# A mixture-of-experts encoder step on one Trainium2 core: row spreading in one pass, banks emptied into a row buffer, a shorter router

## The chip, the cores and the metric

One NeuronCore of a Trainium2 chip (trn2) runs the whole program. The metric is the device time in microseconds, as the median of several executions. PE is TensorE, ACT ScalarE, DVE VectorE, POOL GpSimd and SP the engine whose queue issues most DMAs.

## What is computed

The kernel is one step of a streaming encoder for 256 prompt rows and 32 sample rows (288 in all), width 2048, float32. What matters here is the end of the layer:

```python
x = x + mixed @ w_o                                   # "W_O"
h = rmsnorm(x, norm2_g)
g_idx = argmax(h @ wg + bg)                           # 1 of 4 groups per row
e_val, e_idx = top_k(sub[g_idx], 2)                   # 2 of its 4 experts
combine = one_hot(e_id) * softmax(e_val) * p_g
for e in range(16):                                   # ff = 512
    gate, up = split(h @ wu[e], 2)                    # wu[e]: 2048 x 1024
    out = out + combine[:, e:e+1] * ((silu(gate) * up) @ wd[e])   # wd[e]: 512 x 2048
y = rmsnorm(x + out, final_norm_g)
```

## The kernel before

Five engines run programs of their own, in order, and meet at semaphores only. The dense stages come first: input projections, recurrence, attention, the two gated products (`gated` and `gates`, last of all for `w_pa`), then W_O. The 16 experts follow.

**Precision.** A product keeps float32 accuracy by splitting an operand: ACT writes the rounded high part (`hi`, L893), DVE the remainder (`lo`, L1766 and L1769), and PE runs float32r matmuls over the parts. In the expert stage a 1 MB *piece* of weights is loaded to one of 5 `raw` slots and split in two *halves*; four `sH`/`sL` buffers hold split halves. There are 8 up pieces (U) and 4 down pieces per expert. An up half is 4 matmuls (`up_half`), a split down half (D) 6 (`three`). `NATIVE = [(2, 3)]` names the down pieces that aren't split: for these (N) PE multiplies the raw weights in float32 (`whole`, L1330), and ACT and DVE have nothing to do.

**Order.** `STREAM` is the list of the 192 pieces, made from `PLANS`: string `PLANS[e]` interleaves the U of expert e+1 with the D and N of e; "-" puts in the down pieces of e-1 that are still open. `NTH[t]` counts the split halves ahead of half t. Every engine walks this same list, and other work is tied to places in it (`GL_AT`, `SILU_AT`, `AT_AT`, `ROUND_AT`, `META_AT`, `ROWS_AT`, `DONE_AT`). An engine that waits at one place holds up all that is behind it.

**Groups.** The experts are done in 4 groups of 4. For a group, four *gather* rounds bring its at most 96 rows into `xsH`/`xsL`, and eight *spread* rounds put them transposed into `hgs`, 64 slots per expert: here four rounds for experts 0 and 1, four for 2 and 3, each of 8 matmuls with 128 columns. ACT drains both banks of a round (`drain`). For group g+1 four gathers run while expert 1 of group g has its downs, four spreads at expert 2 and four at expert 3. Group 0 has its four gathers, `meta_turn`, four spreads and `row_turn` ahead of the stream, and four spreads in it.

**An expert's turn.** After its last up half ACT and DVE make the gate and the product (`gl`, `silu`, `actHL`), PE moves them to row order (`remap`, L1412), and ACT and DVE copy them out as `atH`, `atL` (split) and `atF` (for N).

**The end of a group.** The output of a group lies in four PSUM banks `out4`. ACT squares them (`finish`, L960), DVE adds, ACT takes the root (`finish_root`, L965), DVE scales all four banks (`finish_rows`, L1914) and frees them with `yo_ready`; POOL writes the rows with two indirect DMAs. PE waits for `yo_ready` before the next group's first down piece (`residual`, L1405).

**The router.** DVE works on a [96, 3, 20] tile of logits in a chain of small dependent instructions: `first_max` on the group logits, selection of the group's four, `first_max` twice on these. PE then ranks the picks with float32 matmuls (L1305, L1308).

Of the kernel before, what the change touches and what calls it, by code (L numbers as in the profile page):

```python
# [22 lines left out]
P = 128  # L23
D = 2048
KT = D // P
# [60 lines left out]
CUT = [e for e in range(NE) if len(NATIVE[e]) < FM]  # L86
NCUT = [sum(1 for x in CUT if x < e) for e in range(NE + 1)]

# [72 lines left out]
def build(nc, x_prompt, x_sample, cache_k, cache_v, state_conv, state_lru, norm1_g, w_in, conv_w,  # L161
# [19 lines left out]
    ones = sb("ones", [P, P])  # L181
    before = sb("before", [P, P])
# [6 lines left out]
    eps_t = sb("eps_t", [TB, 1])  # L189
    prm = sb("prm", [P, P])  # L190
# [99 lines left out]
    lgT = sb("lgT", [40, T])  # L290
    end2 = here[0]
# [28 lines left out]
    r4 = sb("r4", [TB, 8, FT, 4])  # L320
    r1 = sb("r1", [TB, 6, FT, 1])
    psel = sb("psel", [TB, FT, 4, 4])
    picks = sb("picks", [TB, FT, 20])
# [15 lines left out]
    atH = sb("atH", [P, 2, CAP], F32R)  # L339
    atL = sb("atL", [P, 2, CAP], F32R)  # L340
    atF = sb("atF", [P, FM, CAP])
    end3 = here[0]
    assert max(end1, end2, end3) <= nc.sbuf_usable_end, (end1, end2, end3, nc.sbuf_usable_end)
# [21 lines left out]
    with ExitStack() as ctx:  # L365
        def sem(name):
# [55 lines left out]
                                                    sem("routed"))  # L422
        G_ready, meta_ps, R_ready, idx_ready = sem("G_ready"), sem("meta_ps"), sem("R_ready"), sem("idx_ready")
# [7 lines left out]
        atH_ready, atL_ready = sem("atH_ready"), sem("atL_ready")  # L431
        sqy_ready, ssqy_ready, rmsy_ready, yo_ready = (sem("sqy_ready"), sem("ssqy_ready"), sem("rmsy_ready"),
# [5 lines left out]
        def round_banks(q):  # L438

            if q < 8:  # L440
                return trio[q % 3]
            return pair[0] if q % ROUNDS // 4 == 1 else pair[1]
# [241 lines left out]
        def _(a):  # L684
# [93 lines left out]
            def gates(base, m0):  # L778
                def body(i):
                    for b in range(2):  # L780
# [6 lines left out]
                        a.sem_inc(acc_used[0], 1)  # L787
                        ahead(base, 4, i, 2 * b + 1)
                peeled(a, KT // 2, body)

            gates(T_PB, 0)
# [72 lines left out]
            gates(T_PA, KT)  # L864


            for q in range(4):
                a.wait_ge(mix_ready, KT + 4 * (q + 1))
                a.activation(hH[:, 4 * q:4 * q + 4, :], mixed[:, 4 * q:4 * q + 4, :], ACT.Copy)\
                 .then_inc(mixsplit_s, 1)  # L870
# [37 lines left out]

            a.wait_ge(xr_in, 48)
# [16 lines left out]
            a.wait_ge(logit_ps, KT)  # L926
            a.activation(lgT[:, :], bank[4][0:40, 0:T], ACT.Copy).then_inc(lgT_ready, 1)
            a.wait_ge(ssq_ready, FT + 1)
            a.activation(rms[:, :], ssq[:, :], ACT.Sqrt, bias=eps_t[:, :], scale=1.0 / D).then_inc(rms_ready, 1)
            x1_hi(KT - 1, tail)  # L930

            a.wait_ge(top_ready, 1)
            a.activation(r4[:, 1, :, :], r4[:, 0, :, :], ACT.Exp).then_inc(ge_ready, 1)
            a.wait_ge(dd_ready, 1)
            a.activation(r1[:, 1, :, :], r1[:, 0, :, :], ACT.Exp).then_inc(ed_ready, 1)


            def drain(q, c):

                n, r = q // ROUNDS, q % ROUNDS  # L940
                a.wait_ge((turnA_ps, turnB_ps)[c], q + 1)
                src = round_banks(q)[c]
                if r < 4:
                    a.activation((xsH, xsL)[c][:, 512 * r:512 * (r + 1)], src[0:CAP, :], ACT.Copy)\
                     .then_inc((outA, outB)[c], 1)
                else:
                    k, e = 4 * (r % 4) + 2 * c, 2 * (r // 4 - 1)
                    a.activation(hgs[:, k:k + 2, e:e + 2, :, :].rearrange("p k e h s -> p k (e h s)"),
                                 src[:, :].rearrange("p (k c) -> p k c", k=2), ACT.Copy)\
                     .then_inc((outA, outB)[c], 1)  # L950
# [17 lines left out]
            for q in range(8):  # L968
# [3 lines left out]
            rows(0, bank[6])  # L972
            for i in range(HALVES, NSPLIT):
                for e in range(NE):
# [16 lines left out]
                    if i == AT_AT[e]:  # L991
# [4 lines left out]
                        if e in CUT:  # L996
                            a.activation(atH[:, :, :], src[:, 0:2, :], ACT.Copy).then_inc(atH_ready, 1)
                        m0 = NATIVE[e][0]
                        a.activation(atF[:, m0:, :], src[:, m0:, :], ACT.Copy).then_inc(atF_ready, 1)
                for q, t in enumerate(ROUND_AT):  # L1000
                    if t is not None and i == NTH[t] + 4:
                        drain(q, 0)
                        drain(q, 1)
                for g in range(NG - 1):
                    if i == NTH[ROWS_AT[g]] + 5:
                        rows(g + 1, pair[0][1])
                    if i == NTH[DONE_AT[EPG * g + EPG - 1]] + 3:
                        need(a, y_out, 32 * g)
                        a.wait_ge(eh_done, DONE_AT[EPG * g + EPG - 1])
                        finish(g, g)  # L1010
                    if i == NTH[DONE_AT[EPG * g + EPG - 1]] + 6:
                        finish_root(g, g)
                expert_split(i)
            a.wait_ge(y_out, 32 * (NG - 1))
            a.wait_ge(eh_done, HALF_N)
            finish(NG - 1, NG - 1)
            finish_root(NG - 1, NG - 1)

            a.wait_ge(routed, 1)
            n = a.value_load(cnt_i[0:1, 0:1], min_val=0, max_val=T + ES)  # L1020
            with a.If(n > CAP):
                def again(v, first, width):

                    with a.Fori(0, NG) as g:
# [4 lines left out]
                        with a.Fori(0, width) as w:  # L1029
# [9 lines left out]
                            with a.Fori(0, EPG) as j:  # L1039
                                x = EPG * it + j  # L1040
                                for s in range(PU + PD):
                                    if s == PU:
# [11 lines left out]
                                        a.activation(atF[:, :, :],  # L1054
# [23 lines left out]
        def _(pe):  # L1078
# [221 lines left out]

            pe.wait_ge(picks_ready, 1)
# [748 lines left out]
```

## Time and profile before

| | |
|---|---|
| Median of 3 runs | 1850.07 us (1849.16 to 1851.13) |
| Profiled execution, its own time | 1847.03 us |
| Its span, first to last instruction | 1845.1 us |
| Mean granted TensorE clock | 0.978 |
| PE / DVE / ACT busy | 93% / 61% / 56% |
| Expert stream, first up matmul to last down matmul | 1260.85 to about 1830.4 us |

The span is what the views of the trace show; about 2 us lie outside it. The stream is 31% of the span and has other limits than the stages ahead of it, so it is read by itself.

### The profile page before, as it was taken

The numbers are of one execution on the slowest core, as the hardware profiler recorded it, in microseconds if no ns is written. First come the engines' busy times: TensorE is split into PE (matmuls) and PEld (weight loads), VectorE is DVE, ScalarE is ACT, GpSimd is POOL, SyncE is SP. The second block draws the span as 40 slices with busy tenths as digits, with TensorE's granted clock in tenths as the row PEclk, the third lists the DMA queues.
The fourth block names the chain that finished last, engine by engine and source line by source line (L and its number), as shares of the span: only waits on it lengthen the run. The fifth ranks groups of instructions, "written<-read, shape, count | busy, mean of one in ns | idle before, by whom it ended". The sixth has DMA issues, their size and how long they took to land.

```text
span 1845.1 us, 28902 instructions
## 1 busy us (share of the span) xinstructions
PE 1721.5 (93%) x10867; PEld 1505.3 (82%) x10867; DVE 1120.3 (61%) x1410; ACT 1025.3 (56%) x1500; POOL 134.1 (7%) x176
## 2 busy tenths in 40 slices
PE   5999989999999999999999989988998999899896
PEld 5999989999989888988899989976665676566553
DVE  5888874434444444444344455456887887886883
ACT  6666663333344444344333345557788787787873
POOL 2555430000000000000000000000000000000000
PEclk9999999999999999999999999988999999899898
DMA  7555545566554455445755654525899899899993
GB/s 196 146 171 166 147 140 169 151 180 185 165 172 131 130 173 165 124 141 134 191 162 156 182 174 122 193 99 182 336 373 362 327 378 361 325 372 360 345 389 157
DMA packets 418892, 393.55 MB, mean 213 GB/s; under 512 B 19168, under 2 KB 376896, under 8 KB 409664
## 3 DMA queue, kind: packets, MB, share of 16 engines
q1 hardware_dynamic: 407152, 383.04, 62.3%
q10 hardware_dynamic: 10432, 4.79, 1.0%
q0 software_dynamic: 1232, 4.72, 0.9%
q8 instruction: 46, 0.75, 0.2%
q14 instruction: 30, 0.25, 0.0%
HBM read 385.38 MB, written 11.08 MB: 215 GB/s over the span
## 4 chain that ended last, share of the span: by engine, by line
PE 72%; DVE 11%; ACT 8%; issue 6%; DMA 2%; POOL 1%; ACTq 0%; SPq 0%; DVEq 0%; POOLq 0%
PE bank L1114 13%; PE bank L1115 13%; PE bank L1116 13%; PE bank L1330 5%; PE bank L1337 4%; PE bank L1339 4%; DVE sL L1766 4%; ACT sH L893 2%; PE bank L1277 2%; PE bank L1278 2%; PE bank L1279 2%; ACT wH L691 2%; PE bank L1316 1%; PE bank L1319 1%; PE bank L1322 1%
## 5 line engine op out<-in xcount | busy, mean ns | idle before, releaser
L691 ACT ACTIVATE wH<-ring 128x1024 fp32r<-128x1024 f32 x320 | 335.9, 1059 | 539.5 <-PE bank L1116 479.7
L1557 DVE TENSOR_TENSOR wL<-ring,wH 128x1024 fp32r<-128x1024 f32 x320 | 388.0, 1230 | 375.5 <-ACT wH L691 367.5
L1114 PE MATMUL bank<-hH,wH 128*128 128x288 f32 x1792 | 536.7, 300 | 5.8 <-ACTq L753 2.7
L1115 PE MATMUL bank<-hL,wH 128*128 128x288 f32 x1792 | 530.8, 296 | 0.0
L1116 PE MATMUL bank<-hH,wL 128*128 128x288 f32 x1792 | 530.0, 296 | 0.0
L1766 DVE SCALAR_TENSOR_TENSOR sL<-raw,prm,sH 128x1024 fp32r<-128x1024 f32 x256 | 318.3, 1280 | 84.9 <-ACT sH L893 83.6
L1114 PEld LDWEIGHTS bank<-hH,wH 128*128 128x128 f32 x1792 | 339.2, 189 | 13.0 <-issue 7.0
L1115 PEld LDWEIGHTS bank<-hL,wH 128*128 128x128 f32 x1792 | 339.1, 189 | 0.4
L1116 PEld LDWEIGHTS bank<-hH,wL 128*128 128x128 f32 x1792 | 338.8, 189 | 0.0
L893 ACT ACTIVATE sH<-raw,prm 128x1024 fp32r<-128x1024 f32 x256 | 283.2, 1146 | 56.7 <-PE bank L1339 33.9
L1337 PE MATMUL bank<-sH,hgs 128*128 128x512 f32 x512 | 183.8, 441 | 38.0 <-DVE sL L1766 36.4
L1339 PE MATMUL bank<-sL,hgs 128*128 128x512 f32 x512 | 166.5, 407 | 0.0
L1337 PEld LDWEIGHTS bank<-sH,hgs 128*128 128x128 f32 x512 | 91.6, 196 | 89.2 <-DVE sL L1766 63.1
L1114 PE MATMUL bank<-oH,wH 128*128 128x288 f32 x512 | 150.4, 294 | 3.1 <-DVE oL L1654 3.1
L1115 PE MATMUL bank<-oL,wH 128*128 128x288 f32 x512 | 151.2, 295 | 0.0
L1116 PE MATMUL bank<-oH,wL 128*128 128x288 f32 x512 | 151.0, 295 | 0.0
L1339 PEld LDWEIGHTS bank<-sL,hgs 128*128 128x128 f32 x512 | 100.5, 196 | 24.5
L1330 PE MATMUL bank<-raw,atF 128*96 128x512 f32 x256 | 115.3, 592 | 0.0
L1114 PEld LDWEIGHTS bank<-oH,wH 128*128 128x128 f32 x512 | 96.4, 188 | 3.4 <-issue 3.4
L1115 PEld LDWEIGHTS bank<-oL,wH 128*128 128x128 f32 x512 | 96.4, 188 | 0.0
L1116 PEld LDWEIGHTS bank<-oH,wL 128*128 128x128 f32 x512 | 96.3, 188 | 0.0
L1769 DVE TENSOR_TENSOR sL<-raw,sH 128x1024 fp32r<-128x1024 f32 x64 | 77.9, 1224 | 17.5 <-ACT sH L893 16.8
(309 smaller groups left out, 2141.2 us busy)
## 6 DMA issues: line engine op xcount, KB each, us to landing
raw<-in_expert_w_up SPq DMA_DIRECT2D x128, 1024.0 KB, 7.2
ring<-in_w_in SPq DMA_DIRECT2D x112, 1024.0 KB, 6.0
raw<-in_expert_w_down SPq DMA_DIRECT2D x64, 1024.0 KB, 7.0
ring<-in_w_pb SPq DMA_DIRECT2D x16, 1024.0 KB, 8.5
ring<-in_w_pa SPq DMA_DIRECT2D x16, 1024.0 KB, 8.6
ring<-in_w_o SPq DMA_DIRECT2D x16, 1024.0 KB, 5.5
cK<-in_cache_k SPq DMA_DIRECT2D x16, 256.0 KB, 2.9
cV<-in_cache_v SPq DMA_DIRECT2D x16, 256.0 KB, 3.3
```

The source lines that it names most:

```text
L691: a.activation(wH[2 * (slot % 2) + half][:, :, :], ring[slot][:, 8 * half:8 * half + 8, :], ACT.Copy).then_inc(hi_ready, 1)
L893: a.activation(sH[buf][:, :], raw[slot][:, 1024 * half:1024 * (half + 1)], ACT.Copy, scale=scale)\
L1114: pe.matmul(dst, hi, rH[:, k, :], start=(k == 0), stop=False)
L1115: pe.matmul(dst, hi, rL[:, k, :], start=False, stop=False)
L1116: ins = pe.matmul(dst, lo, rH[:, k, :], start=False, stop=(k == KT - 1))
L1277: pe.matmul(dst, hi, hH[:, k, :], start=(k == 0), stop=False, skip_group_check=True)
L1330: ins = pe.matmul(out4[nb][0:CAP, :], atF[:, m, :], raw[slot][:, nb * 512:(nb + 1) * 512], start=False, stop=stop, skip_group_check=True)
L1337: pe.matmul(banks[c][:, :], w, hi[:, c * 512:(c + 1) * 512], start=(k == 0), stop=False)
L1339: ins = pe.matmul(banks[c][:, :], w, lo[:, c * 512:(c + 1) * 512], start=False, stop=(k == KT - 1))
L1557: v.tensor_tensor(lo[:, :, :], ring[slot][:, 8 * half:8 * half + 8, :], hi[:, :, :].bitcast(F32), ALU.subtract).then_inc(lo_ready, 1)
L1766: v.scalar_tensor_tensor(sL[buf][:, :], src, g2[:, 2 * s + half:2 * s + half + 1], sH[buf][:, :].bitcast(F32), ALU.mult, ALU.subtract).the ...
L1769: v.tensor_tensor(sL[buf][:, :], src, sH[buf][:, :].bitcast(F32), ALU.subtract)\
```

## The change

- `gates` and `gated` take the split of `mixed` for W_O into their last iteration: three quarters ahead of the last product's end, the fourth behind it.
- ACT gets four small activations (`warm`) which place the table of the next function (Sqrt, Exp, Silu, Sqrt) earlier. The copy `lgT` goes from ACT to DVE.
- The router's `first_max` runs on the group logits and on all four groups' logits in one [96, 15, 4] tile: 13 dependent steps to `picks`, on 60 elements a row. `picks`, `ones`, `before` become bfloat16; a semaphore `cnt_ps` of its own follows the three count products.
- A spread round has 4 matmuls with 256 columns, for all four experts and two row blocks. Later groups have all eight spreads at expert 2 of the group before, two halves apart. Group 0 has 4 gathers and 3 spreads ahead of the stream, 5 spreads at halves 2 to 10, and `row_turn` at half 12. `meta_turn` goes ahead of the fourth gather. In the stream's first five spreads ACT drains one bank and DVE the other; for later groups ACT drains both.
- At a group's end ACT squares a bank (`square_bank`) and DVE at once multiplies it by the gain into `yo` (`gain_bank`), which frees it (`scaled_ready`). The root's factor is applied to `yo` afterwards, by ACT on one half and DVE on the other. For the last group banks 0 and 1 start when half a piece is still to come.
- The plans change: a group's last down piece now falls into the next plan, and the six U in a row at a group's start become four with an N among them. The last expert has no N.

```diff
-PLANS = ["UUUUDUDUDUU", "UU-UDUUDUUDU", "UU-UDUUDUUDU", "UU-UDUDUDUDUU"] * NG
-PLANS[NE - 2] = "UU-UDUUUDUU"
-NATIVE = [(2, 3)] * NE
+PLANS = ["UU-UUDUDUDUU", "UU-UDUUDUUDU", "UU-UDUUDUUUD", "UU-UDUUDUUDU"] * NG
+PLANS[0], PLANS[NE - 2] = "UUUUDUDUDUU", "UU-UDUUUDUU"
+NATIVE = [(2, 3)] * (NE - 1) + [()]
...
-ROUND_AT = [None] * 8 + [2, 5, 8, 11]
+FIRST_ROWS = 12
+ROUND_AT = [None] * 7 + [2, 4, 6, 8, 10]
 for _g in range(NG - 1):
-    for _j in (1, 2, 3):
-        ROUND_AT += [DOWN_AT[EPG * _g + _j] + 3 * r for r in range(4)]
+    ROUND_AT += [DOWN_AT[EPG * _g + 1] + 3 * r for r in range(4)]
+    ROUND_AT += [DOWN_AT[EPG * _g + 2] + 2 * r for r in range(8)]
...
+                        if last and b == 1:
+                            for q in range(4):
+                                mixed_hi(q)
                         ahead(base, 4, i, 2 * b + 1)
...
+            a.activation(warm[:, 0:1], eps_t[:, :], ACT.Sqrt)
             a.wait_ge(xr_in, 48)
             part(0)
...
+            def square_bank(g, nb):
+                a.activation(yo[:, 512 * nb:512 * (nb + 1)], out4[nb][0:CAP, :], ACT.Square,
+                             accum_out=ssqy[:, g, nb:nb + 1]).then_inc(sqy_ready, 1)
+            def scale_half(g):
+                a.wait_ge(scaled_ready, 4 * (g + 1))
+                a.wait_ge(root_ready, g + 1)
+                a.activation(yo[:, 1024:], yo[:, 1024:], ACT.Copy, scale=rmsy[:, g, 2:3]).then_inc(yo_ready, 2)
...
                     else:
-                        for kk in range(2):
-                            ins = spread(dst[:, 256 * kk:256 * (kk + 1)].rearrange("p (e h s) -> p e h s", e=2, h=2),
-                                         4 * (r % 4) + 2 * c + kk, 2 * (r // 4 - 1), 2)
+                        ins = spread(dst[:, :].rearrange("p (e h s) -> p e h s", e=EPG, h=2),
+                                     2 * (r - 4) + c, 0, EPG)
...
-            for q in range(4):
-                round(q)
-            pe.wait_ge(meta_ready, 1)
-            meta_turn(0, bank[6])
-            for q in range(4, 8):
+            for q in range(7):
+                if q == 3:
+                    pe.wait_ge(meta_ready, 1)
+                    meta_turn(0, bank[6])
                 round(q)
-            pe.wait_ge(R_ready, 1)
-            row_turn(bank[6], ms[:, 0, 4:9])
...
                 if t == UP_AT[e]:
-                    if j == 0:
-                        pe.wait_ge(outA, ROUNDS * g + 8)
-                        pe.wait_ge(outB, ROUNDS * g + 8)
...
+                    if j == 0 and g > 0 or j == 1:
                         pe.wait_ge(outA, ROUNDS * (g + 1))
                         pe.wait_ge(outB, ROUNDS * (g + 1))
...
                     if j == 0:
-                        need(pe, yo_ready, 4 * g)
+                        if g == 0:
+                            pe.wait_ge(es_ready, 1)
+                        need(pe, scaled_ready, 4 * g)
...
+            def gain_bank(g, nb):
+                v.wait_ge(sqy_ready, 4 * g + nb + 1)
+                if nb == 3:
+                    finish(g, g)
+                c = slice(512 * nb, 512 * (nb + 1))
+                v.tensor_tensor(yo[:, c], out4[nb][0:CAP, :], gain[:, c], ALU.mult).then_inc(scaled_ready, 1)
+            def finish_rows(g):
+                v.wait_ge(rmsy_ready, g + 1)
+                v.reciprocal(rmsy[:, g, 2:3], rmsy[:, g, 1:2]).then_inc(root_ready, 1)
+                v.wait_ge(root_ready, g + 1)
+                v.wait_ge(scaled_ready, 4 * g + 2)
+                v.tensor_scalar(yo[:, 0:1024], yo[:, 0:1024], rmsy[:, g, 2:3], None, ALU.mult).then_inc(yo_ready, 2)
```

## Rows read from the trace of the kernel before

**Rows 1.** The page, busy tenths in 40 slices of 46 us.
```profile
DMA  7555545566554455445755654525899899899993
```

**Rows 2.** What PE waited for, 1258 to 1832 us: total, times, longest.
```profile
PE bank L1337 <- DVE sL L1766: 36.4, 25, 4.0
```

**Rows 3.** Stretches at a group's end: busy PE, PEld, DVE, ACT, POOL, clock, DMA share, GB/s.
```profile
1564.00:1570.00 6.00, 4.01 (x11) 2.89 (x12) 4.45 (x5) 5.95 (x8) 0.00 (x0) 0.79 1.04 414
1570.00:1576.00 6.00, 2.13 (x7) 0.98 (x5) 5.96 (x10) 5.48 (x6) 0.54 (x1) 0.78 0.57 199
```

**Rows 4.** Timeline of PE: remaps of experts 0, 7, 8, 11, 15, and halves between.
```profile
1292.12 0.54 PE L1412 MATMUL bank<-RT,actHL 128*128 128x96 f32 x4
...
1536.57 0.94 PE L1412 MATMUL bank<-RT,actHL 128*128 128x96 f32 x4
...
1581.23 0.55 PE L1412 MATMUL bank<-RT,actHL 128*128 128x96 f32 x4
...
1587.34 0.62 PE L1316 MATMUL bank<-sH,atH 128*96 128x512 f32 x2
...
1588.73 0.63 PE L1337 MATMUL bank<-sH,hgs 128*128 128x512 f32 x2
...
1589.66 0.63 PE L1337 MATMUL bank<-sH,hgs 128*128 128x512 f32 x2
...
1680.21 0.94 PE L1412 MATMUL bank<-RT,actHL 128*128 128x96 f32 x4
...
1814.41 0.62 PE L1412 MATMUL bank<-RT,actHL 128*128 128x96 f32 x4 [0.59 <-DVE actHL L1942]
```

**Rows 5.** Chain that ended last: one spread round.
```profile
1362.45 0.84 PE bank L1373 x8
```

**Rows 6.** Groups of instructions, 1433 to 1577 us: busy, mean ns, idle before.
```profile
L1766 DVE SCALAR_TENSOR_TENSOR sL<-raw,prm,sH 128x1024 fp32r<-128x1024 f32 x65 | 81.1, 1279 | 23.9 <-ACT sH L893 23.6
L893 ACT ACTIVATE sH<-raw,prm 128x1024 fp32r<-128x1024 f32 x64 | 71.0, 1145 | 14.6 <-PE bank L1339 9.7 <-DMA raw<-in_expert_w_up 3.2 <-PE bank L1322 1.4
L948 ACT ACTIVATE hgs<-bank 128x512 fp32r<-128x512 f32 x16 | 8.5, 586 | 0.0
```

**Rows 7.** Timeline at the start of W_O.
```profile
1104.51 0.58 PE L1277 MATMUL bank<-hH,wH 128*128 128x288 f32 x1 [4.98 <-DVE hL L1752]
...
1102.91 5.16 DVE L1752 TENSOR_TENSOR hL<-mixed,hH 128x1152 fp32r<-128x1152 f32 x4
1107.98 1.75 DVE L1759 TENSOR_TENSOR x1L<-xr,x1H 96x1536 fp32r<-96x1536 f32 x1
...
1113.46 0.21 PE L1285 MATMUL bank<-identR,x1H 96*128 96x96 f32 x1
```

**Rows 8.** Timeline of the router.
```profile
1231.32 1.28 ACT L929 ACT_TABLE_LOAD   x1
...
1233.15 0.22 DVE L1812 TENSOR_TENSOR lg<-bank,rstd 96x60 f32<-96x60 f32 x1
...
1237.62 0.20 DVE L1841 TENSOR_TENSOR picks<-picks,r 96x48 f32<-96x48 f32 x1
...
1237.87 0.51 PE L1305 MATMUL bank<-picks,before 96*96 96x20 f32 x2 [5.83 <-DVE picks L1841]
...
1241.30 0.17 DVE L1851 TENSOR_TENSOR pos<-bank,psel 96x12 f32<-96x12 f32 x1 [2.74 <-PE bank L1308]
```

**Rows 9.** Timeline of PE between the router and the stream.
```profile
1251.91 0.30 PE L1373 MATMUL bank<-R,xsH 96*128 96x128 f32 x1 [1.39 <-issue]
...
1260.85 1.19 PE L1337 MATMUL bank<-sH,hgs 128*128 128x512 f32 x2 [1.10 <-ACT RT L954]
```

**Rows 10.** Timeline of the tail.
```profile
1823.38 7.03 PE L1330 MATMUL bank<-raw,atF 128*96 128x512 f32 x16
...
1830.51 0.59 ACT L960 ACTIVATE yo<-bank 96x512 f32<-96x512 f32 x1 [13.89 <-PE bank L1330]
...
1834.75 2.72 DVE L1914 SCALAR_TENSOR_TENSOR yo<-bank,rmsy,gain 96x512 f32<-96x512 f32 x4
```

More of the change, by code:

```diff
@@ L85 @@
 NTH = [sum(1 for x in SPLIT_T if x < t) for t in range(HALF_N + 1)]
-CUT = [e for e in range(NE) if len(NATIVE[e]) < FM]
-NCUT = [sum(1 for x in CUT if x < e) for e in range(NE + 1)]
+NCUT = [FM - len(NATIVE[e]) for e in range(NE)]
 UP_AT = [2 * STREAM.index((e, 0)) for e in range(NE)]
@@ L180, in build @@
     ident = sb("ident", [P, P])
-    ones = sb("ones", [P, P])
-    before = sb("before", [P, P])
+    ones = sb("ones", [P, P], BF16)
+    before = sb("before", [P, P], BF16)
     ident16 = sb("ident16", [P, P], BF16)
@@ L189, in build @@
     eps_t = sb("eps_t", [TB, 1])
+    warm = sb("warm", [TB, 4])
     prm = sb("prm", [P, P])
@@ L775, in _, with gates, body @@
             upper(KT - 1)
-            def gates(base, m0):
-                def body(i):
+            def gates(base, m0, close):
+                def body(i, last=False):
                     for b in range(2):
@@ L930, in _ @@
             x1_hi(KT - 1, tail)
+            a.activation(warm[:, 1:2], eps_t[:, :], ACT.Exp)
+            a.wait_ge(group_ready, 1)
+            a.activation(picks[:, :, 0:4], best[:, 1, :, :].rearrange("p (f g) e -> p f g e", f=FT)[:, :, 0, :],
+                         ACT.Copy).then_inc(pick4_ready, 1)
             a.wait_ge(top_ready, 1)
@@ L935, in _ @@
             a.activation(r1[:, 1, :, :], r1[:, 0, :, :], ACT.Exp).then_inc(ed_ready, 1)
+            a.activation(warm[:, 2:3], eps_t[:, :], ACT.Silu)
             def drain(q, c):
@@ L946, in drain @@
                 else:
[L947 to L950, printed above, removed]
+                    a.activation(hgs[:, 2 * (r - 4) + c, :, :, :].rearrange("p e h s -> p (e h s)"), src[:, :],
+                                 ACT.Copy).then_inc((outA, outB)[c], 1)
             def rows(n, src):
@@ L971, in _ @@
                     drain(q, 1)
-            rows(0, bank[6])
             for i in range(HALVES, NSPLIT):
+                if i == NTH[FIRST_ROWS] + 4:
+                    rows(0, bank[0])
                 for e in range(NE):
@@ L1304, in _ @@
                     lhs = before if e == f else ones
-                    pe.matmul(bank[6][0:TB, f * 20:(f + 1) * 20], lhs[0:TB, 0:TB], picks[:, e, :],
-                              start=(e == 0), stop=(e == f))
+                    ins = pe.matmul(bank[6][0:TB, f * 20:(f + 1) * 20], lhs[0:TB, 0:TB], picks[:, e, :],
+                                    start=(e == 0), stop=(e == f))
+            ins.then_inc(rank_ps, 1)
             for e in range(FT):
@@ L1665, in body @@
                         ahead(base, 4, i, 2 * b)
+                        if last and b == 1:
+                            for q in range(3):
+                                mixed_lo(q)
                         v.wait_ge(half_done, 2 * (base + 2 * m + 2))
@@ L1679, in body @@
                              .then_inc(mix_ready, 1)
+                        if last and b == 1:
+                            mixed_lo(3)
                         ahead(base, 4, i, 2 * b + 1)
-                with v.Fori(i0, i1) as i:
+                with v.Fori(i0, i1 - close) as i:
                     body(i)
+                if close:
+                    body(i1 - 1, True)
             gated(T_PB, 0, False)
@@ L1799, in _ @@
                                 ALU.subtract).then_inc(x1TL_ready, 1)
+            v.wait_ge(logit_ps, KT)
+            v.tensor_copy(lgT[:, :], bank[4][0:40, 0:T]).then_inc(lgT_ready, 1)
             v.wait_ge(sums_ready, FT * KT)
@@ L1849, in _ @@
             v.wait_ge(rank_ps, 1)
             ranks = bank[6][0:TB, 0:FT * 20].rearrange("p (f c) -> p f c", f=FT)
-            own.link(v.tensor_tensor(pos[:, :, :], ranks[:, :, 0:4], psel[:, :, 0, :], ALU.add))
+            own.link(v.tensor_tensor(pos[:, :, :], ranks[:, :, 0:4], off[:, :, :], ALU.add))
             def assign(p, g, done):
@@ L1921, in _ @@
             v.tensor_copy(cnt_i[:, :], cmax[:, :]).then_inc(routed, 1)
-            for q in range(4, 8):
+            for q in range(4, 7):
                 drain(q)
-            columns(bank[6], 0, 0)
             v.wait_ge(gain_in, 16)
             for i in range(HALVES, NSPLIT):
+                for q, t in enumerate(ROUND_AT[:ROUNDS]):
+                    if t is not None and i == NTH[t] + 4:
+                        drain(q)
+                if i == NTH[FIRST_ROWS] + 4:
+                    columns(bank[0], 0, 0)
                 for e in range(NE):
```

249 lines of the change are left out of this document (139 added, 110 removed).

## The prediction

> **What bounds the kernel now.** I read the page's slices first, then the waits of PE, then six-microsecond stretches of the expert stream, and last the timelines of PE, ACT and DVE around the places that the diff touches. In the slices the DMA queues are about half busy in the dense stages, dip at the router, and are at eight or nine tenths in the stream [rows 1]. That could mean a stream bound by transfers. The waits speak against it: PE stood for DVE's split halves in 25 waits, 36.4 us in all, the longest 4.0 [rows 2]. The stretches show where. At a group's end DMA runs at 414 GB/s (1.05 MB in 2.53 us), then falls to 199 GB/s while DVE is busy 5.96 of 6 us, PE 2.13, at a mean clock of 0.78 [rows 3]: ACT and DVE are the bound for a dozen microseconds, once a group.
>
> The remaps give the period. From expert 7's to expert 8's remap 44.66 us pass, from 8's to 11's 98.99 us, three experts [rows 4]. One cycle of four experts is 143.65 us. PE's own work: an up half 0.93 (next start less start), a split down half 1.39 [rows 4], an N half 7.03 / 4, without the modelled overlap 1.72 [rows 10], a spread round 0.84 [rows 5]. Between remaps 7 and 8 lie 13 pieces: 18 x 0.93 + 4 x 1.39 + 4 x 1.72 + 4 x 0.84 + a remap 0.6 = 33.1 us. So 11.5 us are lost there. In an ordinary expert of 12 pieces PE has 28 us of such work, and the 98.99 us hold three of these less a piece (82), four spreads, the gathers, residual, meta and row turns (about 13), so only about 4 us of loss. The stream is PE-bound but for the group's end, and there six U in a row meet the finish work: a U half costs PE 0.93, but ACT 1.1 and DVE 1.2 to 1.3 [rows 6], so PE runs through its four buffered halves.
>
> **Ahead of the stream.** *W_O.* PE waits 4.98 us for the first quarter of `hL` [rows 7]. With the first three quarters split under the last product it starts at 1099.5. The new limit is late in the same product: `x1L`. The last add ends at about 1100.7; ACT's quarter (about 1.1), two split halves (2.1), the Sqrt table that now stands here (1.28 [rows 8] and its small activation), and the `x1H` copy (1.5) lead to about 1106.9, DVE's `x1L` takes 1.75 [rows 7], so the x1 matmuls start at about 1108.6, against 1113.46 [rows 7]. That holds even if the product itself took the 8.95 us of before, part of it at half clock. 4.9 saved; I take 4.5, with 2.5 if the new wait of up to 2.6 us sends the clock down behind it.
>
> *Router.* The table load of 1.28 goes from the path, but DVE's `lgT` copy (0.4) comes ahead of the sum: 1.0. From 1233.15 to the end of `picks` are 4.67 us, 0.5 of them the logits, so some twenty steps at 0.20. Thirteen steps on 60 elements go by the 60-element row, 0.22 plus the gap of 0.03 to 0.06: 3.4, saves 0.8. The ranks take 3.43 us from first matmul to DVE's next [rows 8], nine float32 products at half clock. Now DVE waits for six in one pass. No row shows a bfloat16 product; above is half of 3.43 (1.7), below 0.5 (six starts as close as the trace's closest small ones); I take 0.9, near the low end since 20 columns are little: 2.5. Sum 4.3, range 3 to 5. The added steps for `meta` (about 8 x 0.2) hide under three gather rounds of about 6 us. The Silu warm-up may delay ACT's first gather drain by 1 us, which the third bank pair hides.
>
> *To the first up matmul.* The spread starts 1.39 us after the meta turn, waiting for the one-hots, and the first up matmul follows at 1260.85, 8.94 us after 1251.91 [rows 9]: four rounds at mostly half clock, row turn, two copies. Now the one-hots run under the fourth gather; PE waits 0.75 for its last drain, and does three rounds of 4 matmuls. With 256 columns one has twice the columns of the row and half the instructions, so I put a round at 0.48 full and 0.95 half clock (bounds: 0.42, half the row, and 0.84, the row): 1.5 to 2.9 for three. 1.39 + 8.94 - 0.75 - 2.2 - 0.1 = 7.3 saved, 6 to 8.3. Altogether 16.1 ahead of the stream.
>
> The Trainium skill (ScalarE: Activation LUTs, "What ACT_TABLE_LOAD costs") puts a switch at 1.28 plus 1.38 us of drain. Here the load took 1.28 and the next activation began at once, so the trace does not show the second part. By the page's 2.66 the warm-ups would give about 3 us more over router and tail; the sum here goes by the row.
>
> **Group 0.** From first up matmul to first remap 31.27 us pass [rows 4, 9]. DVE gets five drains (5 x 0.69 = 3.5, at the row of ACT's drain, 0.59, 2.9) and is, with ACT, the bound here (18 splits of 1.2 to 1.3 and 3.4 until its first); ACT loses five drains, so the Silu load saved is on neither's way for sure. Cost 2.0, bounds 0 and 3.5.
>
> **The stream.** Three kinds of interval change, each three times.
> - *Expert 3 to 4 (and 7, 11)*: no spreads, no six U in a row, no finish work until the last piece. PE work 33.1 - 3.4 = 29.8; DVE and ACT have the split work alone, about 28. Transfers: 13 x 2.53 = 33, less what lies in the slots, about two pieces. I take 31.5: 13.2 saved each. Bounds 8 (33 plus a stall of 3) and 14.8.
> - *Expert 2 to 3*: eight spreads in place of four. PE 4 x 0.84 = 3.4 becomes 8 x 0.48 = 3.8. But ACT drains both banks of every one, 16 x 0.53 (0.59 [rows 6] less overlap) in the interval, twice as many as before, and a U piece with a drained round costs it 2.2 + 1.1 = 3.3 against PE's 2.35. Over the eight pieces ACT falls 4 to 5 us behind, the buffers cover 3.7; then PE waits at the next group's first up half for the last drain, which ACT does behind `gl` and `silu`. I take 3.2 lost each, bounds 1 and 6.
> - *Expert 4 to 5*: the finish work. ACT: squares 2.4, two table loads 2.6, root, half of the scaling 1.1; DVE: four gain products at the pace of 2.72 for four [rows 10], its half of the scaling (at most half of 2.72 again). Between the end and the next first down piece PE has four up halves, 3.7 us; the banks are free at about 3.3 and `atL` is ready at about 5. So a stop of 1 us, and the rest lies beside the down pieces, the residual and the row turn, where PE is slower than both. I take 2.1 lost, bounds 0 and 5.
>
> 3 x (13.2 - 3.2 - 2.1) = 23.7 saved. The last group's other intervals change by tenths.
>
> **Tail.** Four N halves (6.9) become four split halves (5.6): 1.3 saved; ACT and DVE can split in time, 2.3 us of their work per half in four buffers. Behind PE's last matmul, at 1830.4, came four squares, a table load, the root, four products up to 1837.5 [rows 10]: 7.1. Now two squares and gains lie under the last half, the table is loaded, and what follows is two squares 1.2, sum, root 0.5, half a scaling 1.1, and the gaps: 3.4. Saves 3.7. Together 5.0, bounds 3.5 and 6.
>
> **Sum.** 16.1 - 2.0 + 23.7 + 5.0 = 42.8, against the profiled execution's 1847.03: 1804.2. The median of the runs is 3.0 above it: **1807 us**.
>
> **Rivals.**
> *A, the forecast*: 1797 to 1818. For it: [rows 4], and that the loss sits in one place. Chance 0.52.
> *B, the stall moves.* ACT is late through the packed spreads, and the finish work lands beside four U; PE stops once in each place for 2 to 4 us and is then at half clock (0.79 and 0.78 in [rows 3]) for several. For it: ACT's arithmetic above. Against: no six U now. At the bounds 8, 6 and 5 the stream gives nothing, at half way to them about 10: 1818 to 1832. 0.20.
> *C, the transfers are the bound.* A piece takes 143.65 / 48 = 2.99 us now; if that were the queues' pace, only the 14 us in front and the 5 behind would stay: 1831. Against: 2.53 us a piece at a stretch [rows 3]. 0.10.
> *D, more.* The stalls go altogether: a cycle at PE's 126 us plus 5: 15 to 20 us better than A, 1787 to 1797. 0.12.
> *E, slower.* PE's wait for the last drain of the eight spreads, at the first up half of each next group: ACT has four splits, `gl` and `silu` ahead of it. It decides if PE stands there for more than 14 us beyond the forecast each time (42.8 / 3); from ACT's rows I get some 3. About 1860. 0.04.
> *F*: the shorter stages end only in other waits, no change: 0.02.
>
> The Trainium skill (TensorE: Matmul & The Clock Gate, "HAM oscillation") warns that recurring idle gaps bring the half clock each time. The stretches at 0.78 agree; under A the gaps get fewer, under B they stay.
>
> No change is within 0.2%, about what a measurement of this kernel can tell: 1846.4 to 1853.8. Faster 0.94 (A to D), same 0.02, slower 0.04. The range 1790 to 1831 leaves out E, F, the low part of D and the high ends of B and C.
>
> **What would show it.** PE's wait at W_O's start gone and one before the x1 matmuls; no table load ahead of the root; under 2 us between last rank input and `pos`; about 4 us from last gather to first up matmul; remap 7 to 8 at 30 to 33 us, 6 to 7 at 35 to 37; squares of banks 0 and 1 ahead of PE's end. I am wrong if the interval with eight spreads is above 40, if the interval behind a group's end is above 38, or if DMA is at 1.0 throughout.

## The result, and the profile after

The kernel after took **1822.65 us** (median of 4 runs, 1819.64 to 1826.64), the one before 1850.60 (4 runs, 1849.16 to 1852.3): ratio 0.985, 95% interval 0.9826 to 0.9874, 28 us faster. The profiled execution took 1820.32 us, its span is 1818.4, its mean clock 0.986. Line numbers below are those of the kernel after: splits L910 and L1809/L1812, up half L1379/L1381, spread L1415, residual L1446, remap L1453, squares L989, gain products L1968.

The page's DMA line (40 slices, here of 45.5 us) is as before in shape, with nine nines in place of eight [rows 1]. PE's waits from 1235 to 1810 us (total, times, longest):

```profile
DMA  8556655657645654663856575536899899999995
```
```profile
PE bank L1379 <- DVE sL L1809: 18.1, 19, 1.8
PE bank L1446 <- DVE atL L2015: 7.6, 4, 2.7
PE bank L1415 <- ACT hgs L968: 5.8, 15, 0.8
PE bank L1453 <- DVE actHL L2008: 3.7, 4, 1.8
PE bank L1379 <- ACT hgs L968: 2.1, 3, 0.7
```

The wait for split halves has halved [rows 2], and a new one, for `atL`, stands before the residual products: 2.67, 2.52 and 2.15 us behind the ends of groups 0, 1 and 2. The timeline of PE, remaps of experts 0, 2, 3, 4, 5 and 15:

```profile
1279.05 0.54 PE L1453 MATMUL bank<-RT,actHL 128*128 128x96 f32 x4
...
1346.79 0.94 PE L1453 MATMUL bank<-RT,actHL 128*128 128x96 f32 x4
...
1382.33 0.94 PE L1453 MATMUL bank<-RT,actHL 128*128 128x96 f32 x4
...
1415.47 0.54 PE L1453 MATMUL bank<-RT,actHL 128*128 128x96 f32 x4
...
1455.15 0.62 PE L1453 MATMUL bank<-RT,actHL 128*128 128x96 f32 x4 [1.77 <-DVE actHL L2008]
...
1793.59 0.62 PE L1453 MATMUL bank<-RT,actHL 128*128 128x96 f32 x4 [0.64 <-DVE actHL L2008]
```

Start less start gives the intervals. All fifteen, before [rows 4] and after, from the same rows of either trace:

```
interval  0-1   1-2   2-3   3-4   4-5   5-6   6-7   7-8   8-9  9-10 10-11 11-12 12-13 13-14 14-15    sum
before  32.56 34.89 32.83 44.65 31.80 34.88 32.84 44.66 31.25 34.88 32.85 44.54 29.63 32.97 27.06  522.29
after   32.57 35.17 35.54 33.14 39.68 36.12 35.85 33.14 37.89 34.57 35.55 33.21 34.56 30.99 26.56  514.54
```

The stall of 11.5 us at 3-4 is gone three times, 34.4 us in all, and four fifths of that are lost again: 2.8 us each at 2-3, and 6.5 on average at 4-5, 8-9 and 12-13, behind the group's end. There the timeline (PE, and `atL` on DVE) and six-microsecond stretches (columns as in [rows 3]) show:

```profile
1420.29 0.36 DVE L2015 TENSOR_TENSOR atL<-bank,atH 128x192 fp32r<-128x192 f32 x1
...
1420.70 1.17 PE L1446 MATMUL bank<-xsH,identR 96*96 96x512 f32 x4 [2.67 <-DVE atL L2015]
```
```profile
1415.47:1421.47 6.00, 3.33 (x16) 2.25 (x15) 6.00 (x10) 6.00 (x12) 0.00 (x0) 1.00 0.99 380
1421.47:1427.47 6.00, 6.00 (x21) 4.23 (x20) 3.77 (x9) 2.21 (x4) 0.00 (x0) 0.55 0.97 340
1427.47:1433.47 6.00, 6.00 (x25) 4.35 (x24) 4.32 (x5) 4.70 (x6) 1.00 (x1) 0.88 0.51 171
```

In the first stretch ACT and DVE are never idle and PE is busy for 3.33 us (it stops for 2.67). In the second it is PE that is never idle, but at clock 0.55, and ACT is busy for 2.21 us only. In the third the DMA share is down to 0.51: PE at half clock has left splits unused, the splits have left slots full, and no transfer could start. The second end (1565.26 to 1571) goes the same way, at 0.54 and 0.50. At the third the clock stays at 1.00 behind a stop of 2.15 us, and DMA stays busy:

```profile
1706.10 1.16 PE L1446 MATMUL bank<-xsH,identR 96*96 96x512 f32 x4 [2.15 <-DVE atL L2015]
```
```profile
1706.10:1709.00 2.90, 2.90 (x13) 2.06 (x14) 2.90 (x3) 2.41 (x3) 0.00 (x0) 1.00 1.04 429
1709.00:1712.00 3.00, 3.00 (x15) 2.25 (x14) 1.80 (x3) 2.07 (x2) 0.00 (x0) 1.00 1.01 289
```

Still 4.9 us are lost at that end (12-13), against 7.9 and 6.6 at the other two: the half clock is a part of the loss, not its condition.

Ahead of the stream, the router and the first spread round behind the last gather:

```profile
1233.64 0.20 DVE L1888 TENSOR_TENSOR picks<-best 96x48 bf16<-96x48 f32 x1
...
1233.99 0.22 PE L1346 MATMUL bank<-picks,before 96*96 96x20 bf16 x1 [3.95 <-DVE picks L1888]
1234.06 0.23 PE L1346 MATMUL bank<-picks,ones 96*96 96x20 bf16 x1
...
1234.65 0.17 DVE L1897 TENSOR_TENSOR pos<-bank,off 96x12 f32<-96x12 f32 x1
...
1245.24 0.36 PE L1415 MATMUL bank<-R,xsH 96*128 96x256 f32 x1 [0.77 <-ACT xsL L965]
...
1246.73 0.63 PE L1379 MATMUL bank<-sH,hgs 128*128 128x512 f32 x2
```

### The profile page after: what moved, and what is told of

Its sections match the earlier page's. It is cut to its first block and busy times, and to the rows that moved or that the text cites. A ratio compares the mean times of both kernels' runs of the same rounds, so it can differ in the third digit from the quotient of the medians.

```text
span 1818.4 us, 28670 instructions
## 1 busy us (share of the span) xinstructions
PE 1703.5 (94%) x10738; PEld 1481.6 (81%) x10738; DVE 1129.2 (62%) x1422; ACT 1032.9 (57%) x1507; POOL 128.7 (7%) x176
## 5 line engine op out<-in xcount | busy, mean ns | idle before, releaser
L1809 DVE SCALAR_TENSOR_TENSOR sL<-raw,prm,sH 128x1024 fp32r<-128x1024 f32 x256 | 317.7, 1280 | 67.4 <-ACT sH L910 66.2
L910 ACT ACTIVATE sH<-raw,prm 128x1024 fp32r<-128x1024 f32 x256 | 283.9, 1152 | 59.2 <-DMA raw<-in_expert_w_up 28.6
L1379 PE MATMUL bank<-sH,hgs 128*128 128x512 f32 x512 | 176.2, 425 | 20.9 <-DVE sL L1809 18.1
L1381 PE MATMUL bank<-sL,hgs 128*128 128x512 f32 x512 | 162.3, 398 | 0.0
L1379 PEld LDWEIGHTS bank<-sH,hgs 128*128 128x128 f32 x512 | 88.4, 190 | 71.3 <-DVE sL L1809 41.0
L1381 PEld LDWEIGHTS bank<-sL,hgs 128*128 128x128 f32 x512 | 96.9, 189 | 23.3
L1372 PE MATMUL bank<-raw,atF 128*96 128x512 f32 x240 | 107.7, 592 | 0.0
L1812 DVE TENSOR_TENSOR sL<-raw,sH 128x1024 fp32r<-128x1024 f32 x68 | 82.5, 1223 | 21.0 <-ACT sH L910 20.4
```

Source lines behind the costliest of these rows:

```text
L910: a.activation(sH[buf][:, :], raw[slot][:, 1024 * half:1024 * (half + 1)], ACT.Copy, scale=scale)\
L1372: ins = pe.matmul(out4[nb][0:CAP, :], at, raw[slot][:, nb * 512:(nb + 1) * 512], start=False, stop=stop, skip_group_check=True)
L1379: pe.matmul(banks[c][:, :], w, hi[:, c * 512:(c + 1) * 512], start=(k == 0), stop=False)
L1381: ins = pe.matmul(banks[c][:, :], w, lo[:, c * 512:(c + 1) * 512], start=False, stop=(k == KT - 1))
L1809: v.scalar_tensor_tensor(sL[buf][:, :], src, g2[:, 2 * s + half:2 * s + half + 1], sH[buf][:, :].bitcast(F32), ALU.mult, ALU.subtract).the ...
L1812: v.tensor_tensor(sL[buf][:, :], src, sH[buf][:, :].bitcast(F32), ALU.subtract)\
```

## The experiments

The profiled executions of after and of the experiments made from it start W_O's x1 products anywhere between 1109.6 and 1115.0 us, though all but `a_best` share the stages up to there; so single times say less than the intervals between remaps. These, for expert 2 to 5 and the three intervals behind a group's end (4-5, 8-9, 12-13), worked out as above:

```
             time    2-3   3-4 |  4-5   8-9  12-13  sum | remap 0-15
before    1850.60  32.83 44.65 | 31.80 31.25 29.63  92.68 | 522.29
after     1822.65  35.54 33.14 | 39.68 37.89 34.56 112.13 | 514.54
a_half    1808.07  35.54 33.15 | 33.53 33.50 32.30  99.33 | 497.27
b_half    1845.99  32.84 44.64 | 31.88 31.32 29.69  92.89 | 518.32
a_oldends 1821.88  35.54 38.12 | 32.57 33.93 32.18  98.68 | 517.63
b_newends 1857.77  33.93 34.77 | 44.44 44.38 40.97 129.79 | 530.63
a_fill    1818.70  35.53 33.13 | 36.15 35.30 35.15 106.60 | 508.81
a_late    1812.74  35.51 33.14 | 34.91 34.77 33.13 102.81 | 505.86
a_late_at 1812.23  35.52 33.13 | 35.90 34.48 32.81 103.19 | 502.47
a_late_half 1801.72 35.52 33.12 | 32.79 32.77 31.62 97.18 | 494.61
a_dve     1829.93  36.70 34.26 | 39.03 40.12 35.65 114.80 | 520.60
a_best    1811.71  35.18 33.14 | 34.63 35.44 33.09 103.16 | 506.26
```

**Half-size transfers, in the kernel after (`a_half`) and before (`b_half`).** Both halves of a piece are computed from the half that is loaded.

```diff
-                    src = up_v[:, e, 2 * s:2 * s + 2, :]
+                    src = up_v[:, e, 2 * s:2 * s + 1, :]
...
-                    src = dn_v[:, e, s - PU:s - PU + 1, :]
+                    src = dn_v[:, e, s - PU:s - PU + 1, 0:1024]
```

> The changed kernel; each expert piece brings only the first half of its columns (0.5 MB), and both halves are computed from it, so the experts' sums are not the reference's; all instructions of PE, ACT and DVE are as they were. Theory Q (ACT and DVE work queued ahead of atL at a group's end, then half clock): the stops stay, only the waits on landings go; 1810 to 1818 us, remap 3 to 7 still above 139 us. Theory D (transfers and their five slots set the pace of a group, 144 us in both kernels): remap 3 to 7 falls to 130 us or less, total 1780 to 1795.

> The kernel before with the same half loads. Theory Q: its loss is the six up pieces and the finish work on ACT and DVE, so remap 3 to 7 stays at 140 to 144 us, total 1840 to 1848. Theory D: remap 3 to 7 falls below 135, total under 1820.

Measured: `a_half` 1808.07 us (2 runs), ratio to before 0.977 (0.9749 to 0.9791); `b_half` 1845.99, ratio 0.9973 (0.9963 to 0.9984). Halving the transfers is worth 17 us of remaps in the kernel after, 13 of them behind the groups' ends (112.13 to 99.33), and nothing in a cycle of the kernel before (its 4 us lie in 13-14 and 14-15), which is what theory Q said of it. For the kernel after neither theory gives the numbers: remap 3 to 7 takes 136.8 us, between the 130 and the 139, and the stops stay but are shorter, 1.32 or 1.33 us each in place of 2.67, 2.52 and 2.15. With landings out of the way the engines alone give about the interval behind an end that I had forecast, 33.5 us, and the stretches behind it are at full clock:

```profile
1420.64:1426.64 6.00, 4.67 (x25) 3.40 (x24) 6.00 (x10) 5.98 (x11) 0.00 (x0) 1.00 0.65 240
1426.64:1432.64 6.00, 6.00 (x29) 4.49 (x29) 5.22 (x12) 4.48 (x6) 0.00 (x0) 1.00 0.56 174
```

The intervals 2-3 and 3-4 don't move by more than 0.01: transfers are not their limit, though DMA stands at a share of 1.01 over 3-4 (403 GB/s, the row of that stretch).

```profile
1382.33:1415.47 33.14, 31.59 (x118) 20.05 (x117) 27.64 (x29) 25.99 (x30) 0.00 (x0) 1.00 1.01 403
```

**The plans and the finish apart: `a_oldends` (old plans at the group's end, all else of after), `b_newends` (before with the new plans there).**

```diff
+PLANS = ["UUUUDUDUDUU", "UU-UDUUDUUDU", "UU-UDUUDUUUD", "UU-UDUDUDUDUU"] * NG   # a_oldends
+PLANS[NE - 2] = "UU-UDUUUDUU"
...
+PLANS = ["UU-UUDUDUDUU", "UU-UDUUDUUDU", "UU-UDUUDUUDU", "UU-UDUUDUUDU"] * NG   # b_newends
+PLANS[0], PLANS[NE - 2] = "UUUUDUDUDUU", "UU-UDUUUDUU"
```

> The changed kernel with the plans of before around a group's end (six up pieces in a row, the group's last down piece inside its own plan), the new finish work and packed spreads kept. Theory M (the plans only moved the stop from the interval ahead of the first remap of a group to the one behind it): remap 3 to 4 back to 40 to 44 us, 4 to 5 back to 32 to 33, total within 5 us of the changed kernel. Rival (the plans are a gain of their own, the finish work cost it): 1832 to 1845.

> The kernel before with only the new plans around a group's end. The first down piece of the next group now comes four split halves behind the end and waits for yo_ready, which DVE gives at its seventh split behind the root: a stop of 6 to 10 us at that place, 3 to 4 at 31 to 33 us. Theory M: 1850 to 1865. Rival (the plans alone bring it): 1825 to 1840.

Measured: `a_oldends` 1821.88 us (4 runs), 0.9842 (0.9824 to 0.986), the same as after. Its loss stands at 3-4 (38.1, under the 40 to 44 expected) in place of 4-5 (32.6). `b_newends` 1857.77 us (6 runs), 1.0038 (1.0026 to 1.0051): slower. The old finish, met earlier, stops PE for up to 6.7 us (PE's waits, 1235 to 1840):

```profile
PE bank L1405 <- DVE yo L1914: 20.1, 3, 6.7
```

The stop and the total are as theory M had them; 3-4, at 34.8, is longer than its 31 to 33. So the new plans alone lose 7 us, and beside the row buffer they neither win nor lose: they move the stop.

**Filling PE's stop (`a_fill`).**

```diff
                 if t == DOWN_AT[e]:
+                    if j == 0 and g > 0:
+                        for _ in range(12):
+                            pe.matmul(pair[0][1][0:CAP, :], identR[0:CAP, 0:CAP], xsH[:, 0:512], start=True, stop=True)
                     pe.wait_ge(atL_ready, e + 1)
```

> The kernel after, with twelve products of 96 x 512 (their result is used by nobody) put ahead of the wait on atL at the first down piece of groups 1 to 3, so that PE does not stand there. If half the loss behind a group's end is the clock (half for some 6 us behind the stop of 2.7 us, which costs about 3.4 us a group), the granted clock stays at full there and the time falls by some 8 to 12 us, to about 1812. If the late transfers set the pace there, the clock stays up as well but PE then waits for the split halves, and the time stays within 2 us of the kernel after's 1822.6. If atL is ready before the added products are through, the time rises by their overhang, at most 1.5 us a group.

Measured: 1818.70 us (4 runs), 0.9838 (0.9822 to 0.9854), 4 us under the kernel after (2 by the ratios of the two to the before of their own batches, whose intervals overlap); in the profiles the remaps take 5.7 us less, 5.5 of them behind the ends. The stretches behind the end:

```profile
1417.71:1423.71 6.00, 6.00 (x29) 4.42 (x28) 6.00 (x9) 5.98 (x13) 0.00 (x0) 1.00 0.95 348
1423.71:1429.71 6.00, 6.00 (x31) 4.55 (x30) 5.23 (x12) 3.97 (x5) 0.00 (x0) 1.00 0.99 366
1429.71:1435.71 6.00, 6.00 (x34) 4.54 (x33) 5.63 (x6) 5.46 (x6) 1.92 (x2) 1.00 0.91 308
```

The clock stays at 1.00, and DMA at 0.91 where it fell to 0.51. PE's residual products start about as long behind the remap as before (5.09 against 5.23 us), so what is saved is the half clock's and its consequences'. It is saved where the kernel after had the half clock: 3.5 us at the first end and 2.6 at the second; at the third, which had none, the interval is 0.6 longer. The 8 to 12 us that I expected did not come, by the time or by the remaps: I had priced 3.4 us at each of three ends.

**A shorter stop: the wait on `atL` behind the residual products (`a_late`), and the copies of `atH`, `atF`, `atL` directly behind squares and gain products too (`a_late_at`).**

```diff
                 if t == DOWN_AT[e]:
-                    pe.wait_ge(atL_ready, e + 1)
                     if j == 0:
...
                         residual(xsH, True, False)
                         residual(xsL, False, False)
+                    pe.wait_ge(atL_ready, e + 1)
...
+                        at_out(EPG * (g + 1))       # a_late_at only: ACT, behind square_bank
...
+                        at_low(EPG * (g + 1))       # a_late_at only: DVE, behind gain_bank
```

> The kernel after, with the copies of atH, atF and atL of a group's first expert issued directly behind the squares and the gain products, and PE's wait on atL moved behind the residual products. If ACT's and DVE's order sets PE's stop, the stop falls from 2.7 us to about 1.2, the clock recovers sooner, and 3 to 9 us are saved in all, to about 1816. If the landings set the pace behind a group's end, what is gained at the stop is lost at the next split halves: under 2 us saved.

> The kernel after with only PE's wait on atL moved behind the residual products; the copies stay where they are. The residual products wait for the last gain product, which ends 1.1 us ahead of atL, and take 1.2 us each for the high and the low part: PE starts some 1.1 us sooner. If it is the length of PE's stop that matters (clock and slots), 1 to 4 us are saved, to 1819 to 1821.5; if the early copies themselves did it (splits behind them sooner), nothing.

Measured: `a_late_at` 1812.23 us (4 runs), 0.9803 (0.9787 to 0.982); `a_late` 1812.74 (4 runs), 0.9803 (0.9788 to 0.9818). One wait moved over two calls saves 9.9 us (8.7 by the ratios), more than the 1 to 4 that I expected: I had counted the 1.1 us and not all that hangs on them. Of `a_late`, timeline and stretches behind the end:

```profile
1422.70 1.16 PE L1446 MATMUL bank<-xsH,identR 96*96 96x512 f32 x4 [0.68 <-DVE yo L1968]
...
1454.46 0.62 PE L1453 MATMUL bank<-RT,actHL 128*128 128x96 f32 x4 [0.27 <-DVE actHL L2008]
```
```profile
1419.55:1425.55 6.00, 5.33 (x29) 3.96 (x28) 6.00 (x10) 5.98 (x11) 0.00 (x0) 1.00 0.95 331
1425.55:1431.55 6.00, 5.90 (x25) 3.83 (x23) 5.87 (x12) 4.69 (x6) 0.00 (x0) 1.00 1.01 406
```

The stops are 0.68, 1.12 and 0.78 us in place of 2.67, 2.52 and 2.15, the clock does not fall, DMA goes on at 1.01, and 4-5 takes 34.91. By ends 4.8, 3.1 and 1.4 us are saved; at the third, where there was no half clock to save, that is the 1.4 us by which the stop is shorter. The early copies add 3.4 us of remaps in the profiles (505.86 to 502.47), but none that the times can tell.

**What is left (`a_late_half`: `a_late_at` with transfers of half the size).**

> The early copies with transfers of half the size in the expert stream (the experts' sums are not the reference's). If landings are what is left of the loss behind a group's end (35.9 us in the interval from expert 4's to expert 5's remap, 34.5 in the last ones), it falls to about 32.5 to 33.5, the remaps from 0 to 15 take about 494 to 497 us, and the time is about 1803. If the engines' order is what is left, it stays near 502 and the time near 1811.

Measured: 1801.72 us (2 runs), 0.9744 (0.9726 to 0.9762); remaps 494.61. As expected for landings: the interval behind an end falls by another 1 to 3 us, to 32.8. The full-size transfers cost `a_late_at` some 8 us of remaps, and 10.5 of the time; no order of the engines that was tried here gives them back.

**ACT's drains at 2-3 (`a_dve`).**

```diff
-                        if q >= ROUNDS:
+                        if q >= ROUNDS and q % ROUNDS < 4:
                             drain(q, 1)
...
-                for q, t in enumerate(ROUND_AT[:ROUNDS]):
-                    if t is not None and i == NTH[t] + 4:
+                for q, t in enumerate(ROUND_AT):
+                    if t is not None and q % ROUNDS > 3 and i == NTH[t] + 4:
```

> The kernel after, with the second drains of the four packed spreads behind the gl product of groups 0 to 2 (12 drains in all) moved from ACT to DVE. In the interval from expert 2's to expert 3's remap ACT is busy without a gap, and the interval is 35.5 us; four drains of 0.55 off ACT make it about 33.5 to 34, and 4 to 6 us fall in all, to about 1818. If the transfers set the cycle, that interval gets shorter by the same but the next ones longer, and the time stays within 2 us of 1822.6.

Measured: 1829.93 us (4 runs), 0.9887 (0.9865 to 0.9909), 7 us slower than after by the medians, with intervals that just overlap; 2-3 grows in all three places, by 0.9 to 1.2 us, to 36.7. Both expectations fail. DVE has the longer split (1.28 against 1.15 us a half), and PE waits 10.6 us for its drains, where it waited 5.8 for ACT's (1245 to 1812):

```profile
PE bank L1415 <- DVE hgs L1954: 10.6, 18, 0.9
```

**Four slots in place of five, after and before.**

```diff
-RAW = 5
+RAW = 4
```

> The kernel after with four slots for landed pieces in place of five. If transfers that start late (a slot comes free late behind a group's end) set the pace, one slot less of 2.5 to 3 us of transfer work makes each cycle markedly longer, 15 to 30 us in all, with most of it in the intervals behind a group's end. If the engines' own order sets it, less than 8 us.

> The kernel before with four slots for landed pieces in place of five. The same edit made the kernel after 47.9 us slower. If the change has brought the transfers from hidden to limiting, the kernel before loses much less by it: 10 to 25 us, to 1860 to 1875. If both hang on the slots alike, it loses some 45 us, too.

Measured: 1870.47 us (4 runs), 47.8 above after, far more than the 15 to 30 expected, and only 10 of the 42 us of remaps lie behind the groups' ends; and 1890.64 (2 runs), 41.2 above the before of its batch (1849.42). The kernel before is nearly as sensitive, so this pair doesn't tell the theories apart: with four slots ACT waits some 90 us for landings in both, from 1245 to 1812 us (91.4 and 87.7, against 28.6 and 17.5 for up pieces with five). More than five slots were not tried.

**W_O's clock, on top of `a_late_at` (`a_best`).**

```diff
+                if m == 0:
+                    for _ in range(20):
+                        pe.matmul(bank[5][:, 0:T], hi, hH[:, KT - 1, :], start=True, stop=True)
                 pe.wait_ge(xL_ready, m // 4 + 1)
```

> The last but one edit (copies of the group's first down piece directly behind squares and gain products), with twenty products of 288 columns, used by nobody, ahead of PE's wait for x1L in W_O's first output tile. If the half clock behind that wait (0.52 for some 3 us) is what W_O gives back, the x1 matmuls come at the same time, the clock stays at full and 1 to 2 us are saved: 1810.5 to 1811.5 against 1812.2. If the twenty products overhang x1L, or the drift of the weights' transfers behind W_O takes it, nothing changes.

Measured: 1811.71 us (5 runs, 1810.07 to 1817.81), 0.9799 (0.9784 to 0.9813): not to be told from `a_late_at`. In the profile the clock stays at 1.00 where it was 0.50.

```profile
1112.00:1115.00 3.00, 3.00 (x25) 2.82 (x23) 2.31 (x2) 1.60 (x2) 0.00 (x0) 1.00 0.56 168
```

From the x1 products to `pos` (starts 1114.51 and 1238.32) pass 123.81 us, against 124.85 (1109.59 and 1234.44) in `a_late_at`: 1.0 saved. Its interval 1-2 took 37.05 in place of 35.17 in that execution; why is open. The version to keep is `a_late`: one line, ratio 0.9803 to before against 0.985 of the kernel after.

## Why the prediction was right or wrong

Spans of the profiled executions fell from 1845.1 to 1818.4, 26.7 us; I had 42.8. The time of 1822.65 lies in the stated range, 15.6 us above the forecast of 1807 and outside A's 1797 to 1818: the range held it because it took in rival B. By its terms:

```
term                   predicted   measured
W_O                        -4.5       -3.3
drift of the dense stages     0       +1.3
router                     -4.3       -4.6
to the first up matmul     -7.3       -7.5
group 0                    +2.0       +1.1
stream                    -23.7       -7.8
tail                       -5.0       -5.9
sum                       -42.8      -26.7
```

**W_O.** The limit is where I put it: PE now waits 2.62 us for `x1L`. From the last product's end (1099.5 before, 1100.8 after, the 1.3 of drift) the x1 products come 5.0 sooner, as forecast. I had 2.5 in case the wait sends the clock down, and it does: the stretch 1112 to 1114 has 0.50. The term was 3.3, between my two values. From the first x1 product to the last group of them pass 116.42 us, 114.79 before: 1.6 given back. In `a_best` it is 114.89, against 116.41 in `a_late_at`, so most of it goes with the clock.

```profile
1109.79 0.31 PE L1325 MATMUL bank<-identR,x1H 96*128 96x96 f32 x1 [2.62 <-DVE x1L L1802]
```
```profile
1112.00:1114.00 2.00, 2.00 (x10) 2.00 (x10) 1.38 (x2) 0.35 (x2) 0.00 (x0) 0.50 0.03 7
```

**Router.** Right. x1 products' last group to `pos` took 13.05 us before and 8.44 after. From the first rank product to `pos` are 0.66 us (1233.99 to 1234.65) in place of 3.43 [rows 8]; I had taken 0.9, near the low end.

**To the first up matmul.** Right: 19.55 to 12.08 us from `pos`. A wait of 0.77 for the last gather's drain (0.75 forecast), then three rounds in 1.5 us, at full clock, where the sum had 2.2. The stretch up to the last gather, which I took as unchanged, is 0.6 longer: two small errors that cancel.

**Group 0.** 32.32 in place of 31.27 us: the cost is 1.05, between my bounds.

**Stream.** Here the prediction failed. I said "3 x (13.2 - 3.2 - 2.1) = 23.7 saved". Measured are 3 x 11.5, 3 x 2.8 and 3 x 6.5, and 1.3 saved in the other intervals.
- *3-4* went from 44.65 to 33.14; I took 31.5, and not for the reason that I feared. Not the transfers (`a_half` has 33.15): PE waits 1.6 us for `sL` and is busy for 31.59, where I had counted 29.8. Part of that looks like DVE's pace and not PE's own: PE's weight loads wait for `sL` for 3.9 us in 6 waits, and up halves start up to 1.20 us apart (1389.77 and 1390.97), not 0.93.
- *2-3* was nearly right, 35.54 for 36.0, and ACT, with sixteen drains, is busy for 31.29 us of it, against 27.47 of 32.83 before. That the drains are the whole cost isn't shown: with four of them on DVE (`a_dve`) the interval gets longer, not shorter.
- *4-5* is the failed step: "I take 2.1 lost, bounds 0 and 5"; lost were 7.9, 6.6 and 4.9. Its arithmetic of the engines holds once the landings don't interfere: `a_half` gives 33.5, 1.7 lost, with a stop of 1.32. I wrote "So a stop of 1 us": it was 2.67, 2.52 and 2.15. Two things were left out. First, the transfers: with the stall at 3-4 gone they run at 403 GB/s up to the group's end and come late, ACT stands 1.76, 1.53 and 1.14 us for a landing just ahead of the three ends (row below: the first), and squares, gain products and `atL` are late behind the splits. Second, what the stop set off at two of the three ends: half clock over the next 6 us, slots that stay full, an idle DMA, and late landings once more.

```profile
1409.90 2.20 ACT L910 ACTIVATE sH<-raw,prm 128x1024 fp32r<-128x1024 f32 x2 [1.76 <-DMA raw<-in_expert_w_up]
```

The 19.45 us behind the three ends come apart as follows. Half clock and what follows from it: 5.5 (`a_fill`), all of it at the first two ends. The stop, cut to about 1 us, with them: 9.3 (`a_late`). Landings, with all of it: 12.8 (`a_half`), and with the shorter stop 15.0 (`a_late_half`, where 4.5 are left). The shares overlap, since each sets off the next.

**Tail.** Right: 24.81 in place of 30.69 us from remap 15 [rows 4, 10]. The table load is hidden, the squares of banks 0 and 1 lie ahead of PE's end at about 1806.6:

```profile
1802.34 1.28 ACT L1050 ACT_TABLE_LOAD   x1
...
1805.41 0.59 ACT L989 ACTIVATE yo<-bank 96x512 f32<-96x512 f32 x1 [1.57 <-PE bank L1364]
...
1809.10 1.15 ACT L996 ACTIVATE yo<-yo,rmsy 96x1024 f32<-96x1024 f32 x1 [0.46 <-DVE rmsy L1973]
```

**The rivals.** What happened is B, given 0.20: "PE stops once in each place for 2 to 4 us and is then at half clock". It stops so in one of the two places, behind the group's end, and is at half clock behind two stops of three; for the spreads' banks it waits 0.8 at the longest. My sum for B was wrong: the bounds 8, 6 and 5 give 3 x (8 - 6 - 5) = -9 and not nothing, and half way to them the stream gives 7 and not 10, so by the rest of the sum B is 1824 half way and 1840 at the bounds, not 1818 to 1832. C is in it as the reason why ACT and DVE are late, not as a bound by itself: the stream moved by 7.8 us, and DMA falls idle behind two of the three ends (0.51, and 0.32 from 1574 to 1577). E's mechanism, PE behind the last of eight drains, cost 2.1 us in three waits, 0.7 the longest (fifth row of PE's waits above). I named as proof against me "if the interval behind a group's end is above 38", and it was 39.68 once.

The Trainium skill (TensorE: Matmul & The Clock Gate, "HAM oscillation") says of its example, in which PE waits for DMA in every iteration, that the half clock comes back each time. Here it comes back in part: behind two of the three stops at the groups' ends, not behind the third, of 2.15 us. `a_late`, whose stops there are 0.7 to 1.1 us, shows full clock in every six-microsecond stretch from 1280 to 1790 us.

## What to carry to other kernels

A stall that is taken away lets the transfers catch up with the engines: cost the next tight place with landings late by a microsecond or two, not with the engines' own work alone. Before work is made faster at a place where PE waits for two things, look which of the instructions behind the wait need only one of them: here one wait moved over two calls was worth 9 to 10 us, a third of the whole change. A stop can cost more than its length: shortened by 2.0 us at the first end it gave back 4.8 (`a_late`), but 1.4 for 1.4 at the third, where no half clock had followed.

## What was not expected of the hardware

- The clock does not answer to stops of like length alike. PE stopped for 2.67 us and then had 0.55 over six microseconds; for 2.52 us, and had 0.54 and 0.50; for 2.62 us in W_O, and had 0.50; for 1.77 us at 1455.15, and had 0.56 from 1457 to 1460. But behind 2.15 us at 1706.10 it kept 1.00, as behind 1.96 us in `a_best` (1594.30) and 2.05 us in the kernel before (1421.67). Behind stops of 0.68 and 1.26 us (`a_late`, `a_late_at`) it kept 1.00. What decides between them stays open.
- A half clock isn't always paid for. In group 0 PE stops for 1.80 us in the kernel after (to 1270.27) and in `a_half` (to 1275.45); the same stretch behind it is at 0.50 in the one and at 1.00 in the other (rows below, after and `a_half`). From first up matmul to first remap both take the same time, 32.32 and 32.33 us: DVE is busy for the whole stretch in both.

```profile
1272.00:1275.00 3.00, 2.77 (x8) 1.58 (x6) 3.00 (x5) 2.82 (x4) 0.00 (x0) 0.50 0.84 255
```
```profile
1277.00:1280.00 3.00, 1.95 (x8) 0.95 (x6) 3.00 (x4) 2.82 (x4) 0.00 (x0) 1.00 0.61 175
```

- Bfloat16 products of 20 columns start 0.08 us apart at the router (1233.99, 1234.06, 1234.14), at a clock of 0.50.
- The stages ahead of W_O took up to 5 us more or less in executions of kernels that share them (x1 products from 1109.6 to 1115.0 us). What sets that stays open.
